# RWKV stage of a fused block: a pair's modulation products between the scan's steps, in another PSUM bank

## The reference

```python
def adaln_mod(cond, w, b):                       # first block
    m = jnp.einsum('...d,de->...e', jax.nn.silu(cond), w) + b
    return jnp.split(m[..., None, :], 6, axis=-1)

# second block
mod = jax.nn.silu(c) @ mod_w[l] + mod_b[l]       # 1 x 1024 by 1024 x 6144

# RWKV branch, per head, per direction, over the tokens
sa = jnp.einsum('bhvk,bhk->bhv', s, -kk_t)
s = s * w_t[:, :, None, :] + sa[..., None] * (kk_t * a_t)[:, :, None, :] + v_t[..., None] * k_t[:, :, None, :]
y = jnp.einsum('bhvk,bhk->bhv', s, r_t)
```

## Time and profile before

| | |
|---|---|
| median of three runs | 3788.46 us |
| the three runs | 3788.17, 3788.46, 3794.42 us |
| span of the profiled execution | 3791.7 us |
| RWKV stage in it | 88 to 1026 us |
| PE, DVE, ACT busy | 87%, 40%, 27% of the span |
| TensorE's time in the 64 `modulate` calls of the stage | 47.3 us (512 recorded matmuls) |

### The profile page before, as it was taken

How to read it: one execution, slowest core, us unless ns; L and a number is a source line. 1 busy time by engine, 2 the same in 40 slices (tenths; PEclk the granted TensorE clock), 3 DMA queues, 4 the chain that set the end, 5 groups by cost and what they waited for, 6 DMA issues and landing times. The chain is left out here.

```text
span 3791.7 us, 55933 instructions
## 1 busy us (share of the span) xinstructions
PE 3314.0 (87%) x23810; PEld 2001.2 (53%) x23810; DVE 1503.3 (40%) x3077; ACT 1018.1 (27%) x1973; POOL 56.6 (1%) x73
## 2 busy tenths in 40 slices
PE   7888999888799999699976787788999999869995
PEld 3566666666655555444442232244545555458884
DVE  3666676766457567500032101022333242331113
ACT  2343344343124554500020000022333423101101
POOL 0000000000000000000000000000000000000000
PEclk9999999999799999799988999998999999959997
DMA  4112222211311221232048999922111110358873
GB/s 170 56 55 72 69 63 79 64 52 52 112 53 61 78 94 52 103 133 111 16 157 356 431 431 431 431 98 106 47 67 47 67 40 8 117 208 336 334 312 150
DMA packets 104317, 542.23 MB, mean 143 GB/s; under 512 B 30256, under 2 KB 33056, under 8 KB 79904
## 3 DMA queue, kind: packets, MB, share of 16 engines
q1 hardware_dynamic: 97184, 513.86, 35.2%
q0 software_dynamic: 4608, 16.78, 1.2%
q10 hardware_dynamic: 2304, 8.39, 0.5%
HBM read 511.54 MB, written 27.45 MB: 142 GB/s over the span
## 5 line engine op out<-in xcount | busy, mean ns | idle before, releaser
L2355 PE MATMUL mh_ps<-mh_w_ahead,xmT 128*128 128x512 f32 x768 | 336.6, 593 | 0.0
L2087 PE MATMUL ex_ps<-ex_ring,ex_xs 128*64 128x512 f32 x1024 | 241.3, 627 | 66.2 <-DMA ex_ring<-expert_slabs_in 63.1
L492 PE MATMUL rw_ps<-hT,rw_w 128*128 128x512 f32 (+1 forms) x640 | 259.7, 536 | 6.1 <-PEq L61 5.8
L2994 PEld LDWEIGHTS ge_ps<-ge_xeT,ge_ring 128*128 128x128 f32 x2048 | 233.0, 193 | 10.5 <-issue 10.5
L2994 PE MATMUL ge_ps<-ge_xeT,ge_ring 128*128 128x128 f32 x2048 | 233.3, 276 | 2.9 <-DVE ge_xeT L3052 2.9
L2355 PEld LDWEIGHTS mh_ps<-mh_w_ahead,xmT 128*128 128x128 f32 x768 | 144.9, 191 | 167.3 <-issue 165.2
L2087 PEld LDWEIGHTS ex_ps<-ex_ring,ex_xs 128*64 128x64 f32 x1024 | 87.0, 144 | 220.0 <-issue 220.0
L1257 PE MATMUL sg_ps<-hTp,sg_w 128*128 128x512 f32 x384 | 170.5, 597 | 0.0
L492 PEld LDWEIGHTS rw_ps<-hT,rw_w 128*128 128x128 f32 x640 | 113.1, 192 | 89.5 <-issue 79.8
L2339 PE MATMUL mh_ps<-xmT,mh_w_ahead 128*128 128x512 f32 x256 | 127.4, 632 | 14.3 <-PEq L61 8.0
L2087 PE MATMUL ex_ps<-ex_ring,ex_hidT 128*64 128x512 f32 x512 | 118.3, 617 | 13.8 <-DMA ex_ring<-expert_slabs_in 12.5
(11 more groups left out here) (574 smaller groups left out, 5388.6 us busy)
## 6 DMA issues: line engine op xcount, KB each, us to landing
ex_ring<-expert_slabs_in SPq DMA_DIRECT2D x96, 2048.0 KB, 18.1
ge_ring<-expert_slabs_in SPq DMA_DIRECT2D x48, 2048.0 KB, 12.1
mh_w_ahead<-head_slabs_in SPq DMA_DIRECT2D x16, 2048.0 KB, 7.6
rw_mod_w<-mod_w_in SPq DMA_DIRECT2D x64, 384.0 KB, 4.1
rw_mod_w<-ada_in SPq DMA_DIRECT2D x64, 256.0 KB, 3.3
sg_kern<-cum_dram SPq DMA_DIRECT2D x64, 256.0 KB, 3.3
rw_w<-rw_slabs_in SPq DMA_DIRECT2D x8, 1536.0 KB, 6.6
sg_w<-xbc_blocks_in SPq DMA_DIRECT2D x24, 512.0 KB, 5.1
```

Source lines behind the costliest of these rows:

```text
L492: mm = pe.matmul(where[j, part], w[:, k, P * j:P * j + P], tokens, start=k == 0, stop=k == KC - 1)
L2087: mm = pe.matmul(ps[halves[j], bank, :], src[:, k, halves[j]], ring[:, (n + j) % RING, k, :], start=k == 0, stop=k == KC - 1)
L2355: mm = pe.matmul(ps[:, 4 + t, :], xmT[:, k, P * t:P * t + P], w[:, slot, k, :], start=k == 0, stop=k == KC - 1)
L2994: mm = pe.matmul(ps[:, 2 + 2 * (j % 2) + n, P * f:P * f + P], w[:, k, P * f:P * f + P], xeT[:, j, k, :], start=k == 0, stop=k == KC - 1)
```

## The change

All eight `modulate` calls leave PE's front. Calls 0 and 1 now stand between the new-part products and the gate product, calls 2, 3, 4 and 5 behind the scan's steps 5, 6, 8 and 9, and calls 6 and 7 behind step 11, directly before the next pair's `near`. They write bank 2, since bank 1 holds the next pair's value projection by then. Bank 2 held the next pair's r projection, so calls 0 and 1 wait for `shifted_r`, and the third group of the next `near`, which writes bank 2, waits for DVE's add (`mod_done`). The add itself moves on DVE from behind the first `exponents` to between `fill(p, 1)` and the readout's reduction, and PE's old wait for it before `mr` goes. On SP, `next_pair(c + 2)` (parameters, low-rank weights and the 1.5 MB weights of a pair) moves from behind the row's stores and bias loads to directly behind load 7.

```diff
-        SCAN, Y, MOD, GATE, YT = (7, 0), 4, 1, 5, 4
+        SCAN, Y, MOD, GATE, YT = (7, 0), 4, 2, 5, 4
...
@sync
+                    if c + 2 < PAIRS:
+                        next_pair(c + 2)
                     sp.wait_ge(s.mod_done, c + 1)
                     for row, _, out in mod_parts(c):
                         sp.dma_start(out, row).then_inc(s.mod_stored, 16)
                     if c + 1 < PAIRS:
                         mod_bias(c + 1)
-                    if c + 2 < PAIRS:
-                        next_pair(c + 2)
...
@tensor, near
                     for g in range(3):
+                        if g == MOD and c:
+                            pe.wait_ge(s.mod_done, c)
...
@tensor, main loop
                     if core:
-                        modulate(c, 0)
                         keys(c, 3)
-                        modulate(c, 1)
...
                         keys(c, 4)
-                        modulate(c, 2)
...
                         keys(c, 5)
-                        modulate(c, 3)
                         value_part(c)
-                        modulate(c, 4)
...
                         join_first(c)
-                        modulate(c, 5)
...
                         join_second(c)
-                        modulate(c, 6)
-                        modulate(c, 7)
...
                         wu(c, 0)
                         wu(c, 1)
-                        pe.wait_ge(s.mod_done, c + 1)
...
                         new_part(c)
+                        if prep:
+                            pe.wait_ge(s.shifted_r, p + 1)
+                        modulate(c, 0)
+                        modulate(c, 1)
                         pe.wait_ge(s.mr_kept, 6 * c + 6)
...
                             scan_step(c, step)
                         if prep and step <= 4:
                             project_part(2, 1, 2 * step - 2, 2 * step)
+                        if core and step in (5, 6, 8, 9):
+                            modulate(c, step - 3 if step < 7 else step - 4)
+                    if core:
+                        modulate(c, 6)
+                        modulate(c, 7)
                 turn_y(LAST)
...
@vector, main loop: these three lines move from behind exponents(p, 0) to behind fill(p, 1)
                         dve.wait_ge(s.mod_bias, NMOD * (c + 1))
                         dve.wait_ge(s.mod_used, KC * (c + 1))
                         dve.tensor_tensor(mrow[:, :], ps[:, MOD, 0:MW], mrow[:, :], ALU.add).then_inc(s.mod_done, 1)
```

More of the change, by code:

```diff
@@ L990, in _ @@
                         exponents(p, 0)
[L991 to L994, removed]
                     if prep:
@@ L1050, in _ @@
                     if core:
+                        dve.wait_ge(s.mod_bias, NMOD * (c + 1))
+                        dve.wait_ge(s.mod_used, KC * (c + 1))
+                        dve.tensor_tensor(mrow[:, :], ps[:, MOD, 0:MW], mrow[:, :], ALU.add).then_inc(s.mod_done, 1)
                         dve.wait_ge(s.y_done, c + 1)
```

## The result

The kernel after took 3818.95 us in the median of four executions (3814.28 to 3824.48), against 3790.60 (3788.17 to 3794.42) for the kernel before: a ratio of 1.0072, 95% interval 1.0058 to 1.0087. That is slower, by 28 us, and outside the predicted range. The profiled execution took 3814.28 us with a span of 3812.5, 20.8 more than before's. The last pair's output leaves the RWKV stage at 1048.65 us in it, against 1022.06 before: 26.6 us later. The other stages differ by 5.8 us the other way, and executions of one kernel spread by more than that. So all of the loss is in the RWKV stage, and the rest of the text speaks of that stage.

A forecast was written before the change was run, and what follows sets the result against it. PE sets the pace on average, DVE's chain in some places. Seven pairs at -1.4 us (-9.8) plus +8.2 for the last pair gave -1.6 on 3788.46, put at 3787 us; range 3781 to 3795, with rivals 3775 to 3799.

The forecast's parts named there:

- front without its products: PE from key products to w/u: removing the products starts w/u and all behind it 3.3 us earlier a pair.
- clock in front of w/u: PE before the w/u products: no clock loss was counted, 0 us a pair.
- clock behind the gate: Four products behind the gate: clock stays high with 1.2 us of idle left, saving 1.2 us a pair.
- products in the scan: Scan steps 5 to 11: two-slot loads at 4.5 us a hop leave 1.1 of 4.5 us gained before `near`.
- clock at `near` and the key products: Around `near`: clock falls again, low part perhaps shorter; 0.3 us a pair saved, bounds 0 and 1.3.
- the last pair: Last pair, no next pair's work as cover: readout's reduction 8.0 us later, plus 0.2 for low clock: +8.2 us.
- rival 2: Scan: the two-slot ring is the bound; hop 5.0 and product 5 or 7 at half clock, +13 us, 3801; chance 0.13.
- the rival that rested on it: Scan loads land sooner than any row shows: at a hop of 3.4, -17 us, 3771; chance 0.02.
- the gate not delayed: Before the gate product: products 0 and 1 (1.3 us) fit into 2.5 us of waiting; 1.2 us remain.
- SP's queue: SP behind load 7: next pair's parameters and slab, then stores and bias loads, go out later; cost 0.
- the other bank: PSUM bank 2: DVE has drained it long before the gate; cost 0.
- About 30 us: PE in the scan: waits for modulation loads before products 4 to 7, about 30 us over eight pairs.

The follow-up runs named there:

- e4: Kernel after without any modulation product or load for one (the row keeps only its biases): 3788.21 us against 3789.47 for the kernel before, ratio 0.9995.
- e1: Kernel after without loads 2 to 7 of each pair; products 2 to 7 reread the two slots: 3772.90 us against 3789.47 for before, ratio 0.9957.
- e5: Kernel after with four load slots instead of two, loads 4 and 5 going into the pair's weights `w`: 3786.64 us against 3790.34 for before, ratio 0.9989.
- e6: Kernel after, two slots, products 2 to 7 moved behind scan steps 2, 3, 5, 6, 9 and 11: 3793.84 us against 3790.34 for before, ratio 1.0011.
- e10: Kernel after with only the 256 KB half of each load after the first two: 3782.92 us against 3788.70 for before, ratio 0.9990.
- e3: Kernel after plus two useless products a pair where products 6 and 7 stood, before `kk_sums`: 3810.46 us, ratio 1.0054 to before.
- e9: As e4, plus four useless products a pair, two before `kk_sums` and two before the gate product: 3759.51 us against 3788.70 for before, ratio 0.9918.
- e2: Kernel after with SP's `next_pair(c + 2)` put back behind the row's stores and bias loads: 3822.18 us, ratio 1.0089 to before.
- e7: As e6, with two value-projection pieces moved from between the w/u products to both sides of `kk_sums`: 3792.71 us against 3790.34 for before, ratio 1.0007.
- e11: Kernel after with e5's four slots, e7's moved value-projection pieces and the last pair in the old order: 3775.64 us against 3788.70 for before, ratio 0.9964.
- e12: Kernel after with e6's places, e7's moved value-projection pieces and the last pair in the old order: 3779.41 us against 3788.70 for before, ratio 0.9979.

## Why the prediction was wrong, step by step

| a pair, us | forecast | measured |
|---|---|---|
| front without its products (measured: e4's 50.89 against 54.29) | -3.3 | -3.4 |
| clock in front of w/u | 0 | +1.5 |
| clock behind the gate | -1.2 | -0.4 |
| products in the scan | +3.4 | +5.9 |
| clock at `near` and the key products | -0.3 | -1.1 |
| sum | -1.4 | +2.5 |
| seven pairs | -9.8 | +17.8 |
| the last pair | +8.2 | +8.8 |
| stage | -1.6 | +26.6 |

**"The products in the scan" is the step that failed; rival 2 came true in its mechanism.** The ring of two slots was there, with the chain 3, 5, 7 ending last and `near` directly behind it. The term was mis-sized: 3.4 us a pair forecast, 5.9 measured. The rows of the seven pairs split the 2.5 us between them. The two hops from product 3 to product 7 take 5.4 us each in the mean, where the sum had 4.5: 1.75 us. Product 5 runs at half clock in five pairs, wholly or in part: 0.33. And so does product 7, directly in front of `near`: 0.40. In pair 2 the hops are 5.81 and 4.48 us, in the last pair 5.4 and 5.1. So the hops are the larger part and the clock, which falls in the waits themselves, the smaller.

The prediction took a hop from loads that mostly flew alone, when the old places kept them apart. In the new order the loads of products 4 and 5 are issued 1.75 us apart, and the second half of load 5 landed 5.0 us after its issue in the mean of seven pairs, that of load 4 4.1. The trace of the kernel before had this too, in loads that nothing waited for: a pair's loads 0 and 1 go out 1 to 2 us apart (behind the output stores of the pair before), and in pairs 1 to 7 the second half of load 1 took 4.8 to 6.5 us to land, that of load 0 4.1 to 5.9, and load 1's took longer each time. The rival had both parts of the truth, a hop of 5.0 and a product at half clock; it was given 0.13, and its price of +13 us was less than half of the +28 measured, as it had no clock lost in front of w/u and kept the 1.2 us at the gate. e1 shows the term by itself (25.00 to 20.36), e5 and e6 that most of it goes when a product stands further from the release of its load, and e10 that it goes with fewer bytes and one issue less.

The Trainium skill (DMA: Bandwidth & Descriptors, "Anatomy of one DMA") would give an estimated 2.9 us for 384 KB, by a fit for the GpSimd path. The rows here, of loads issued by SyncE behind a 256 KB one, have 4.0 to 5.3, so the trace doesn't bear it out for them, and the rival that rested on it is refuted. The same page ("Rules for kernel authors") says that transfers issued by different engines run on the same 16 DMA engines and interleave. Both loads here are SyncE's, so the 5.31 us of the overlapped load are in keeping with shared engines, but don't test that sentence.

**The clock in front of w/u was not foreseen.** The prediction gave 3.3 us for the front and took them as final. The removal did bring them (e4: 3.4, with 0.59 us of waiting for ACT before `kk_sums` in it, as it said). What it did not ask is what PE does while it waits: 1.07 us of idle time in two pieces around twelve tiny matmuls, then the 1.2 GHz level and 1.3 us more for the w/u products. Products 6 and 7 had covered just these pieces. e3 and e9 show it by putting work without use there. It costs 1.48 x 7 = 10.4 us.

**"No fall at the gate" was right, its worth was not.** The clock is at 1.00 behind the gate in all seven pairs. But before it had fallen there in only two of them: gate to scan step 1 is 2.75, 2.75, 4.05, 2.74, 2.74, 2.75 and 3.99 us. The prediction read the third, 3.19 us for four products, and multiplied it by seven; the rows of one pair do not look like those of the next there. It is 0.4 a pair, not 1.2: 7 x 0.84 = 5.9 us of the miss came from one row that was not typical.

**The clock at `near`** fell as expected in seven of eight pairs, but earlier in the cycle: in three of the seven steady ones the key products already run at full clock, and w/u comes 1.5 us sooner (49.57 from the first key product instead of 51.08). At 1.1 us a pair (0.35 before the key products, and 4.10 - 3.40 = 0.70 behind) it was within the bounds of 0 and 1.3.

**Right:** the gate not delayed (1.29 us of waiting left, 1.2 forecast); SP's queue at no cost in the time (e2); nothing lost by the other bank (no sign in any wait, and e1 keeps it); `near` directly behind product 7. The last pair, +8.8 for +8.2, is right only as a sum: it reaches the gate 1.3 us earlier (0.4 forecast) and needs 10.2 us more from there on. "About 30 us" of waits for loads were 37.2, not far off; the cycle was 115.5 us instead of 111.5.

**Open.** Medians and stage ends agree within some 6 us and not better, and e7 against e6 is 10.2 us in the profiles and 1.1 in the medians. The profiled executions are single ones: those of the kernel after, e7, e10, e11 and e12 are the fastest of theirs, those of e1, e3, e4 and e9 the slowest, so splits of a pair say where time went in that execution and not exactly how much in the median. e10 changes bytes and one issue together, so their shares in a hop are not told apart. And why the clock falls behind a wait in one pair and not in the next, with the same rows around it, no run shows.

## What to carry to other kernels

In a ring of two slots, what counts is the distance between consumers against the load as it flies in the new order, not in the old: moving consumers close together makes their loads overlap, and each then takes longer. Before pricing a removal, look at what the removed work covered: idle pieces under 1 us can cost more in clock than the work did, and then a piece of other work has to go into them (e7, e11). And read a clock term over all repetitions of a loop before multiplying it.

## What the runs showed of the hardware

- Taking 47.3 us of PE's work out changed the time by nothing measurable (e4), and putting four of the eight products of a pair back, without use, made the kernel 29 us faster (e9). The granted clock accounts for nearly all of it: w/u to gate 27.63 against 25.86 us, gate to scan step 1 4.38 against 2.74, together 3.4 of the 3.5 us a pair.
- Two idle pieces of 0.59 and 0.48 us with twelve two-column matmuls of 1.5 us between them were followed by the 1.2 GHz level in all seven pairs of after, e1 and e4 (w/u in pair 2: 3.25, 3.52 and 3.26 us instead of 1.96). It isn't certain each time: one pair in e2 and one in e5 kept the full clock (1.96 us) behind the same two pieces.
- The length of a wait alone does not tell. Behind 2.50 us before the gate the clock fell in two of seven pairs (before), behind 2.49 us in one of seven (e11), two of seven (e12) and three of seven (e7), behind 2.65 us in all seven (e4), and behind 1.3 us in none (after, e1, e3, e9).
- Two loads of 640 KB issued 1.75 us apart: the product that waited for the first started 4.07 us after the issue of its second half, the one that waited for the second 5.31. Where each load was 256 KB alone, its landing took 3.0 us in the median (e10), and with 384 KB issued behind it 3.5 (after).
